# Three down-projection stages by seven block products in place of eight, for five of sixteen tile pairs

## What is computed

```python
hn = rms_norm(h, norm_ffn[i])                              # h: 256 x 2048
h = h + jnp.square(jax.nn.relu(hn @ ffn_w1[i])) @ ffn_w2[i]   # w1: 2048 x 8192, w2: 8192 x 2048
gate = jax.nn.sigmoid(rms_norm(h, norm_ple[i]) @ ple_w_gate[i])
h = h + (p[i] @ ple_w_proj[i]) * gate
```

## Time and profile before

| | before |
|---|---|
| median of 3 runs | 2210.34 us |
| span of the profiled execution | 2209.0 us (no time of its own beside the span was recorded for it) |
| TensorE busy | 2197.2 us, 99% |
| VectorE busy | 1445.2 us, 65% |
| ScalarE busy | 1106.9 us, 50% |
| GpSimd busy | 550.7 us, 25% |
| one down stage of chunks 0 to 2 | 87.06 us |

### The profile page before, as it was taken

One profiled execution on the slowest core, in us unless ns is written; L12 is line 12 of the kernel. 1 busy time (PEld: TensorE's weight loads), 2 busy tenths in 40 slices (PEclk: granted clock), 3 DMA queues, 4 the chain that ended last, 5 costly groups with the idle time before them and its releaser, 6 DMA issues.

```text
span 2209.0 us, 34195 instructions
## 1 busy us (share of the span) xinstructions
PE 2197.2 (99%) x11625; PEld 1878.9 (85%) x11625; DVE 1445.2 (65%) x1925; ACT 1106.9 (50%) x1654; POOL 550.7 (25%) x531
## 2 busy tenths in 40 slices
PE   9999999999999999999999999999999999999998
PEld 7888988888888888888888887888888888888887
DVE  6877765555664565555566667567785688756875
ACT  6445555453453454445455455565553455534553
POOL 3202220350240141053000033005540245403431
PEclk9999999999999999999999999999999999999999
DMA  7675335556555555556555653545555555555554
GB/s 254 232 230 163 115 128 204 170 190 208 191 190 192 189 189 192 186 192 193 187 185 179 227 171 135 193 160 188 195 188 196 192 183 192 189 195 192 186 209 149
DMA packets 118072, 414.21 MB, mean 188 GB/s; under 512 B 12896, under 2 KB 18048, under 8 KB 117472
## 3 DMA queue, kind: packets, MB, share of 16 engines
q1 hardware_dynamic: 111600, 401.37, 53.9%
q10 hardware_dynamic: 6384, 11.70, 1.7%
HBM read 409.29 MB, written 2.15 MB: 186 GB/s over the span
## 4 chain that ended last, share of the span: by engine, by line
PE 98%; DVE 1%; ACT 1%; issue 0%; DMA 0%; DVEq 0%; ACTq 0%
PE bank L486 33%; PE bank L494 17%; PE bank L543 7%; PE bank L545 7%; PE bank L544 7%; PE bank L1059 4%; PE bank L1060 4%; PE bank L1061 4%; PE bank L599 1%; PE bank L601 1%; PE bank L600 1%; PE bank L619 1%; PE bank L994 1%; PE bank L656 1%; PE bank L796 1%; PE bank L798 1%
## 5 line engine op out<-in xcount | busy, mean ns | idle before, releaser
L1100 DVE TENSOR_TENSOR wboth<-raw,wboth 128x1024 fp32r<-128x1024 f32 x756 | 982.2, 1302 | 607.8 <-ACT wboth L1802 607.1
L1802 ACT CAST wboth<-raw 128x1024 fp32r<-128x1024 f32 x756 | 790.9, 1049 | 711.5 <-PE bank L545 241.6
L486 PE MATMUL bank<-A,wboth 128*128 128x512 f32 x2928 | 705.1, 391 | 0.3 <-DVE wboth L1100 0.3
L486 PEld LDWEIGHTS bank<-A,wboth 128*128 128x128 f32 x2928 | 537.0, 188 | 104.6 <-issue 1.0
L494 PEld LDWEIGHTS bank<-A,wboth 128*128 128x128 f32 x2928 | 376.7, 191 | 14.8
L494 PE MATMUL bank<-A,wboth 128*128 128x256 f32 x2928 | 384.0, 283 | 0.0
L543 PE MATMUL bank<-wboth,H 128*128 128x512 f32 x576 | 224.6, 390 | 0.0
L545 PE MATMUL bank<-wboth,H 128*128 128x512 f32 x576 | 224.2, 389 | 0.0
L544 PE MATMUL bank<-wboth,H 128*128 128x512 f32 x576 | 224.1, 389 | 0.0
L2257 POOL TENSOR_TENSOR bias<-z,rs 128x256 f32<-128x256 f32 x64 | 75.7, 1182 | 481.2 <-DVE z L1131 391.6
L2257 POOL TENSOR_TENSOR PT<-z,rs 128x256 f32<-128x256 f32 x88 | 73.4, 835 | 465.4 <-DVE z L1131 464.8
(11 more groups left out here) (293 smaller groups left out, 2409.1 us busy)
## 6 DMA issues: line engine op xcount, KB each, us to landing
raw<-wstream SPq DMA_DIRECT2D x756, 512.0 KB, 3.3
bias<-bias_rows ACTq DMA_DIRECT2D x6, 512.0 KB, 5.4
x<-xrows ACTq DMA_DIRECT2D x1, 2048.0 KB, 10.0
bias<-grows ACTq DMA_DIRECT2D x2, 1024.0 KB, 6.1
out<-x SPq DMA_DIRECT2D x8, 256.0 KB, 2.1
x<-xT SPq DMA_DIRECT2D x7, 256.0 KB, 4.6
pA<-bias_rows ACTq DMA_DIRECT2D x2, 512.0 KB, 8.9
Sm<-grows ACTq DMA_DIRECT2D x1, 1024.0 KB, 5.8
```

The source lines that it names most:

```text
L486: last = nc.tensor.matmul(bank(j)[:, :], whi[:, s, cols(i)], moving(j, k), start=(k == 0), stop=(k == K - 1))
L1100: V.tensor_tensor(wlo[:, s, :], raw[:, s, :], whi[:, s, :].bitcast(F32), ALU.subtract).then_inc(lo_ready, 1)
L1802: C.copy(whi[:, s, :], raw[:, s, :]).then_inc(hi_ready, 1)
```

## The change

The down stages of chunks 0, 1 and 2 are written anew (chunk 3 stays). Column groups are taken in pairs (`down_pair`): a piece now holds one hidden tile for two column groups, and a pair is 16 pieces. Two neighbouring tiles x and y, two token halves and two column groups make a 2x2 by 2x2 block product, 8 block products. For tile pairs 3 and 5 of the first pair of column groups and for 1, 3 and 5 of the second (`FAST`) it is done by seven, from sums of weight tiles and of hidden tiles. Such a group begins at piece 6, 10, 18, 22 or 26 of the stage (`X_AT`). TensorE gathers four main banks and four side banks; the main banks of one pair are the side banks of the other.

New work: GpSimd makes the sums of hidden tiles (`mix`, in the up stage) with their low parts (`mix_low`) and adds the corners to x (`corners`). ScalarE makes the high parts of the sums (`mix_high`, `t_highs`) and copies one side bank (`copy_side`). VectorE makes four 512-column weight sums per group (`t_first`, `t_second`) and their low parts, two 1024-column differences (`t_lows`), and adds banks to x (`sides_in`, `mains_in`). Of tile x of a group only half the piece is split. The load of `gfrow` moves from the attention to just ahead of `proj`, `proj` uses the other banks first, and GpSimd's loop over four units is written out. Weights are laid out by `pairs` for these chunks.

```diff
+FAST = ((3,5),(1,3,5))
+MIXED = sorted({m for ms in FAST for m in ms})
+GROUPS = [(cp, n, m) for cp, ms in enumerate(FAST) for n, m in enumerate(ms)]
+X_AT = {16 * cp + 2 * m: g for g, (cp, n, m) in enumerate(GROUPS)}
...
+        def main_bank(cp, j):
+            return psum[(UB["fd0"] + j) % 4] if cp else psum[4 + j]
+        def side_bank(cp, j):
+            return main_bank(1 - cp, j)
...
+                def group(i, g):
+                    _, n, m = GROUPS[g]
+                    lone, final = n == 0, n == len(FAST[cp]) - 1
+                    if lone and cp == 0:
+                        pe.wait_ge(z_ready, z0)
+                    if lone and cp:
+                        pe.wait_ge(*banks_taken.at(c * 8 + 4))
+                    product(side_bank(cp, ONE), *hidden(i, early), *weights(i, 0), lone, final).then_inc(piece_used, 1)
+                    arrive(i + 1)
+                    product(main_bank(cp, 0), *hidden(i + 1, early), *weights(i + 1, 0))
+                    pe.wait_ge(*mix_ready.at(c * len(MIXED) + (MIXED.index(m) + 1)))
+                    product(main_bank(cp, 2), *mix_of(m, 3), *weights(i + 1, 1)).then_inc(piece_used, 1)
+                    pe.wait_ge(*t_lo.at(2 * group_of(c, g) + 1))
+                    product(side_bank(cp, FIVE), *mix_of(m, 1), *sums(0), lone, final)
+                    product(side_bank(cp, SEVEN), *mix_of(m, 0), *sums(1), lone, final)
+                    pe.wait_ge(*t_lo.at(2 * group_of(c, g) + 2))
+                    product(side_bank(cp, SIX), *mix_of(m, 2), *sums(2), lone, final)
+                    product(main_bank(cp, 1), *hidden(i + 1, late), *sums(3)).then_inc(t_used.sem, 1)
...
VectorE:
             def rows_body(p, p0, per, groups, evac, between={}, short=0, ahead={}, halves=()):
                 for q in range(LEAD, per * groups + AHEAD):
+                    if q in ahead:
+                        ahead[q]()
                     if AHEAD <= q < per * groups + AHEAD - short:
+                        split_lo(p + q, (p0 + q) % SLOTS, WIDE if q in halves else PW)
                     if q - LEAD in between:
                         between[q - LEAD]()
...
+            def down_pairs(c, fd, o):
+                steps_of.update({x - 4: lambda x=x, g=g: t_first(c, x, g) for x, g in X_AT.items()})
+                steps_of.update({x - 3: lambda x=x, g=g: t_second(c, x, g) for x, g in X_AT.items()})
+                ahead = {x + 2: lambda g=g: t_lows(c, g) for x, g in X_AT.items()}
+                steps_of.update({12: lambda: sides_in(c, 0), 17: lambda: mains_in(c, 0, range(4)), 28: lambda: sides_in(c, 1),
+                                 30: lambda: mains_in(c, 1, range(2)), 31: lambda: mains_in(c, 1, range(2, 4))})
+                rows_body(p, PB[fd], 32, 1, lambda f: None, steps_of, 0, ahead, X_AT)
...
+            def mains_in(c, cp, js):
+                if cp == 0:
+                    dve.wait_ge(piece_used, o * 64 + (PB[fd] + SLOTS + 16))
+                    dve.wait_ge(z_ready, o * 24 + (4 + UB[fd] + 4))
+                    dve.wait_ge(*corners_added.at(c * 6 + 3))
...
+                for j in js:
+                    dst = quarter(cp, j % 2, j // 2)
+                    V.tensor_tensor(dst, dst, main_bank(cp, j)[:, :], ALU.add).then_inc(z_ready if cp else banks_taken.sem, 1)
...
ScalarE:
+                steps_of.update({n: lambda n=n, m=m: mix_high(c, n, m) for n, m in enumerate(MIXED)})
+                steps_of.update({x - 2: lambda g=g: t_highs(c, g) for x, g in X_AT.items()})
+                steps_of.update({12: lambda: copy_side(c, 0), 28: lambda: copy_side(c, 1)})
...
-                    act.dma_start(gfrow, grows[0].partition_broadcast(P)).then_inc(in_gf, 16)
...
+            act.wait_ge(*t_used.at(group_of(FF_CHUNKS - 1, 0)))
+            act.dma_start(gfrow, grows[0].partition_broadcast(P)).then_inc(in_gf, 16)
...
GpSimd:
+                    if 2 * it + 1 in MIXED and not is_last(c):
+                        mix(c, MIXED.index(2 * it + 1), it)
+                if not is_last(c):
+                    for n, m in enumerate(MIXED):
+                        mix_low(c, n, m // 2)
+                    for cp in range(2):
+                        corners(c, cp)
```

More of the change, by code:

```diff
@@ L253, in program @@
         tA, tB, tC = ring(Sm, 0), ring(Sm, 4 * S), ring(Sm, 8 * S)
+        Tsum = ptf.rearrange("p (n c) -> p n c", n=4)
+        Tcopy = [Tboth[:, h, :, :] for h in range(2)]
+        tCf = tC.rearrange("p n w -> p (n w)")
+        corner, cross = tCf[:, 0:WIDE], tCf[:, WIDE:2 * WIDE]
+        mixsum = kT[:, :, :, :].rearrange("p a g c -> p (a g c)")[:, 0:3 * WIDE].rearrange("p (n i q) -> p n i q", n=3, i=4)
+        mixed = [vT[:, 0:3, :].rearrange("p n (i q) -> p n i q", i=4),
+                 mixlo[:, 4 * S:4 * S + 3 * WIDE].rearrange("p (n i q) -> p n i q", n=3, i=4)]
         ub, c0 = ring(ptf, 0, 4, S + 4), ring(ptf, 4 * (S + 4), 2)
@@ L829, in chunk @@
                 else:
-                    with pe.Fori(0, 2) as it:
-                        for f in range(2):
-                            down(it, f)
+                    for cp in range(2):
+                        down_pair(c, cp)
             def turn_fd(f):
@@ new lines, in t_second, with t_lows @@
+            def t_second(c, i, g):
+                y = raw[:, (PB["fd0"] + i + 1) % SLOTS, :]
+                dve.wait_ge(*t_sum.at(2 * group_of(c, g) + 1))
+                V.tensor_tensor(Tsum[:, 2, :], Tsum[:, 0, :], y[:, WIDE:], ALU.add).then_inc(t_more.sem, 1)
+                dve.wait_ge(*t_more.at(2 * group_of(c, g) + 1))
+                V.tensor_tensor(Tsum[:, 3, :], Tsum[:, 2, :], y[:, 0:WIDE], ALU.add).then_inc(t_more.sem, 1)
+            def t_lows(c, g):
+                for h in range(2):
+                    two = slice(2 * h, 2 * h + 2)
+                    dve.wait_ge(*t_hi.at(2 * group_of(c, g) + (h + 1)))
+                    V.tensor_tensor(Tcopy[1][:, two, :], Tsum[:, two, :], Tcopy[0][:, two, :].bitcast(F32), ALU.subtract).then_inc(t_lo.sem, 1)
@@ new lines, in sides_in @@
+            def sides_in(c, cp):
+                _, fd, o = chunk_at(c)
+                done = banks_taken.sem if cp else z_ready
+                dve.wait_ge(*t_used.at(group_of(c, len(FAST[0]) + (len(FAST[1]) if cp else 0))))
+                if cp or not is_chunk(c, 0):
+                    dve.wait_ge(*corners_added.at(c * 6 + 3 * cp))
+                one, five, six, seven = (side_bank(cp, j)[:, :] for j in range(4))
+                V.tensor_tensor(quarter(cp, 1, 0), quarter(cp, 1, 0), seven, ALU.add).then_inc(done, 1)
+                V.tensor_tensor(quarter(cp, 1, 1), quarter(cp, 1, 1), seven, ALU.subtract).then_inc(done, 1)
+                dve.wait_ge(*side_copied.at(c * 2 + (cp + 1)))
+                V.tensor_tensor(quarter(cp, 0, 0), quarter(cp, 0, 0), one, ALU.add).then_inc(done, 1)
+                V.tensor_tensor(corner, six, cross, ALU.subtract).then_inc(side_step.sem, 1)
+                dve.wait_ge(*side_step.at(c * 2 + (cp + 1)))
+                V.tensor_tensor(cross, corner, five, ALU.subtract).then_inc(done, 1)
@@ L2298, in chunk @@
                 ff, fd, o = chunk_at(c)
-                with pool.Fori(0, 4) as it:
+                for it in range(4):
                     for j in range(4):
-                        i = c * 16 + it * 4 + j
-                        take(o * 24 + it * 4 + UB[ff], ZB["ff0"], j, mul(zr[:, j, :], rs[:, :]))
+                        i = c * 16 + (it * 4 + j)
+                        take(o * 24 + (it * 4 + UB[ff]), ZB["ff0"], j, mul(zr[:, j, :], rs[:, :]))
                         pool.wait_ge(ff_relu, i + 1)
```

176 lines of the change are left out of this document (155 added, 21 removed).

## The result

The changed kernel takes 2225.72 us (median of 4 runs, 2224.76 to 2226.25), the kernel before 2210.41 (4 runs, 2210.3 to 2210.77). The ratio is 1.0066, 95% interval 1.0053 to 1.0078: slower by 0.66%. I had put 2212.5 as the time, 2206 to 2219 as the range, and 0.39 on slower; the range doesn't hold it.

A forecast was written before the change was run, and what follows sets the result against it. The prediction took TensorE alone to bound the three down stages. From 2210.34 us it took 10.2 for removed products and added 9.3 for piece-18 waits and 3.0 in chunk 0: +2.1, 2212.5 us, range 2206 to 2219.

The forecast's parts named there:

- Removed products: Down stages of chunks 0 to 2: 45 fewer matmuls at 0.2267 us each, 10.2 us less.
- Prices of VectorE's operations and its order up to piece 18: Pair two's first group waits for VectorE's queued additions to x: 3.11 us per chunk, 9.3 us more in all.
- the sum: Main forecast for the whole kernel: -10.2 + 9.3 + 3.0 = +2.1, 2212.5 us; chance 0.42 as it stands.
- Chunk 0 at piece 7: Late VectorE and GpSimd's three lows make TensorE wait 2.3 us; with what carries on, 3.0 us more in chunk 0.
- They cost nothing in chunks 1 and 2, where it enters on time: Pair one's corner additions on GpSimd fall into VectorE's spare time; VectorE's difference of piece 4 starts 4.0 us into the stage.
- Rival (b): GpSimd's up-stage mixes make VectorE late in chunks 1 and 2 too: 2.3 + 3.8 us per chunk, 2218.5; chance 0.15.
- The clock: TensorE's clock in the three 2.8 us idles at piece 18: no cost in the main forecast, a fall only in a rival.
- Rival (a): TensorE's clock falls in the three piece-18 gaps: 1.1 to 3.3 us each, taken 4 in all, 2216.5; chance 0.32.
- The cases as exclusives: Whole kernel: main forecast and three rivals treated as alternatives, with chances 0.42, 0.32, 0.15 and 0.11.
- GpSimd's turns: GpSimd and VectorE take turns, the loser waiting a whole instruction: 2212.5 us with turns, 2209.5 without.
- Free edits: Swapped `proj` banks, side additions and unrolled loops: no added wait or gap expected.

## Why the prediction was wrong, point by point

*Removed products*: right. 45, at 0.2267 us each: stages without a wait come out at 84.32 with 12 fewer.

*Prices of VectorE's operations and its order up to piece 18*: right. The chain was written down from the code and priced at 3.11 us; 3.17 was measured where nothing else disturbs, released by the operation named. In the changed kernel it is 3.23, 3.86 and 4.09, so the 0.7 us that the sum let chunk 0 carry on to piece 18 are 0.06 there and 0.7 and 0.9 in the two chunks where it had none. Without the lows, and so without the waits at piece 7, chunk 0 does carry 0.8; in the changed kernel TensorE has by then lost 4.1 us itself, behind piece 7. The 0.7 and 0.9 are gone when the lows are.

*Chunk 0 at piece 7*: right in cause and, for the wait, in size, 2.42 against 2.3. Forecast in the form "GpSimd's three lows between VectorE's operations"; without the lows it vanishes.

*"They cost nothing in chunks 1 and 2, where it enters on time"*: wrong, and this is the first step that failed. VectorE does not enter on time there: its difference of piece 4 starts 8.0 us into the stage and not 4.0, and with the three lows behind it the two chunks lose 1.16 and 1.11 us at piece 7 and 0.7 and 0.9 more at piece 18 than the 3.17 of the undisturbed chain. I compared the mix (about 2 us) with GpSimd's pause of 2.26 us per unit and found room. That pause belongs to the fast rhythm of the up stage, and the stage isn't in it any more: from its second unit on, before any mix, GpSimd's product takes 1.65 us and the pause is 1.92. The same in the kernel without mixes, where the entry is at 5.8. In this rhythm a mix, which took 0.75, 1.32 and 0.46, 2.65 us in all from 652.57 to 655.22, overruns the pause, and each of the three puts GpSimd 0.75 us back. Rival (b) had the late entry right and its reason, the mixes, for a part only; chunk 0's rhythm stood there as evidence, with 0.15. What puts chunk 1 into the slow rhythm is not shown: the corners of the stage before run into its first unit in every version here, and none moves those of the second pair. I had priced the corners against VectorE alone, not against GpSimd's own next stage. (b)'s price, 2.3 + 3.8 per chunk, was too high at piece 7 (1.1 measured) and right at piece 18 (3.9, 4.1).

*The clock*: the second step that failed, in the sum rather than in the mechanism. Rival (a) said what happened, and its bounds of 1.1 to 3.3 per gap hold it: 1.4 and 1.7 in chunks 1 and 2, 2.9 in chunk 0. But it stood beside the sum as another case, with 0.32, and the sum put the clock at nothing, where 7.6 us were measured, the largest single miss. The sum itself forecast gaps of 2.8 us, and the earlier trace rows had the clock gone after 2.2 idle: on that evidence a fall was the likelier outcome of the sum's own gaps, and its price belonged in the sum. Nor did I put it on the piece-7 wait of chunk 0, since each idle there is short (0.48 and 1.50 us); the fall behind it cost 1.7.

*The cases as exclusives*: with both rivals on top of each other the prediction's own terms give -10.2 + 18.3 + 4 = 12.1 more, 2222.5, near the 2225.7 measured. The range ended at 2219, just above (b) alone at 2218.5, and left (a)'s own dear end, 2212.5 + 10, outside. That the sum's 2.1 more came out as 15.3 is so for the most part the clock (7.6), then chunks 1 and 2 (2.3 at piece 7, 1.6 at piece 18, less 0.7 in chunk 0 that did not come), then the up stage (0.9).

*Up stage of chunk 0*: not in the sum, 0.9. The mixes were costed at nothing there, by cover that chunk 0's rhythm doesn't have: behind that of tile pair 1 GpSimd's next product comes 7.04 us after the last, 6.23 without it.

*GpSimd's turns*: right as a mechanism; the waits at piece 7 and what chunks 1 and 2 carry on from there hang on it. The Trainium skill (SBUF — State Buffer, section "SBUF: two separate sides") has the loser of the shared ports wait for a whole instruction; the 1.78 instead of 0.68 of a sum beside a low or a corner agree. I priced it for chunk 0 only.

*Free edits*: right as far as shown; none was undone by itself. TensorE waits nowhere for the swapped banks, `gfrow` or a loop's end; 0.33 us at chunk 3's start, for an addition of VectorE, was not forecast.

## What to carry to other kernels

When a forecast contains an idle of the bounding engine, the price of what idleness does to its clock goes into the same sum; a rival is what would happen instead, not as well. Before adding work to an engine's pause, look whether its loop can run in a slower rhythm, with a shorter pause, beside an engine with which it takes turns: compare with a stage of the same kernel that is already in it, and look at what the new work in front of the loop does to its first turn. And where an operation releases a bank, write out its engine's queue and move it to the first place that its inputs allow: one step was worth 16.6 us here, more than all that the change removes.

## What the runs showed of the hardware

- The clock of TensorE fell in gaps of very different shape, and not in all of one shape. Idle for 2.94 us it stayed at 2.4 GHz in chunk 0 and, idle for 2.93, fell to 1.2 in chunk 1 of the same execution (no sums of hidden tiles). Idle for 0.48 and 1.50 us with three products between, it fell. Idle once for 1.05 to 1.90 us at piece 18 (six gaps of the two versions with another order of the mixes) it stayed. What tells the two equal gaps apart I did not find.
- At half clock the same product starts every 0.43 us instead of 0.23. A fall cost 1.4 to 2.9 us, in addition to the gap, behind idles of 2.9 to 3.8. In chunk 2 of the changed kernel the slow products began only 1.0 us behind the gap's end.
- A wait of TensorE for VectorE costs up to 0.25 us beside the wait itself: 0.05 to 0.15 from the end of VectorE's operation to the first product, 0.08 to 0.11 more up to the second.
- Three GpSimd operations of 512 columns took 5.7 to 6.8 us beside a busy VectorE, about twice the 1.02 each that the earlier trace rows has. A VectorE sum beside one took 1.78 us instead of 0.68.
- One and the same loop of short GpSimd and VectorE operations ran in two rhythms: GpSimd's product 0.74 us with a pause of 2.26 before it (chunk 1 before), or 1.65 with 1.92 (chunk 1 after, and without mixes too), to the end of the stage.
